# The last feed forward of a two-block network: seven of its eight upward weight groups as 2x2 block products, seven products for eight

## The reference, cut to what matters

```python
def squared_relu_mlp_2(h, w1, w2):
    return jnp.square(jax.nn.relu(h @ w1)) @ w2
...
        hx = modulate(rmsnorm(x, norm2_g[layer]), sh2, sc2)
        x = x + g2 * squared_relu_mlp_2(hx, w_mlp1[layer], w_mlp2[layer])
...
    return rmsnorm(x, final_g)
```

## Time and profile before

| | us |
|---|---|
| median of three runs | 3636.82 |
| lowest, highest | 3636.82, 3644.08 |
| span of the profiled execution | 3635.2 |
| PE busy in it | 3455.9 (95%) |
| the chain that ended last: PE's part | 88% |
| last feed forward, PE's part of the chain, 3253.80 to 3615.07 | 361.27 |
| ACT, DVE, POOL busy in the whole span | 1205.8, 2014.6, 226.8 |

### The profile page before, as it was taken

One profiled execution on the slowest core, in us unless ns is written; L12 is line 12 of the kernel. 1 busy time (PEld: TensorE's weight loads), 2 busy tenths in 40 slices (PEclk: granted clock), 3 DMA queues, 4 the chain that ended last, 5 costly groups with the idle time before them and its releaser, 6 DMA issues.

```text
span 3635.2 us, 42169 instructions
## 1 busy us (share of the span) xinstructions
PE 3455.9 (95%) x17456; PEld 2750.8 (76%) x17456; DVE 2014.6 (55%) x3705; ACT 1205.8 (33%) x2017; POOL 226.8 (6%) x314
## 2 busy tenths in 40 slices
PE   7989999999989999998999889999998998799998
PEld 6647688887867688887986567888886885478886
DVE  5564587896664578884125675333335235664334
ACT  5353432225453332223112233332333212243332
POOL 0200000001040000000000001000001000000000
PEclk9999999999999999999999799999999999889999
DMA  5302144442212154443210021122122310113331
GB/s 169 103 18 92 63 157 152 162 139 87 75 29 81 53 168 162 154 147 128 80 62 28 9 80 47 59 60 68 59 66 80 112 59 30 41 58 95 98 97 58
DMA packets 210011, 317.00 MB, mean 87 GB/s; under 512 B 5304, under 2 KB 154426, under 8 KB 208540
## 3 DMA queue, kind: packets, MB, share of 16 engines
q1 hardware_dynamic: 194012, 243.00, 20.8%
q0 software_dynamic: 15808, 71.31, 5.8%
HBM read 300.66 MB, written 14.49 MB: 87 GB/s over the span
## 4 chain that ended last, share of the span: by engine, by line
PE 88%; DVE 8%; ACT 3%; issue 1%; DMA 0%; SPq 0%; DVEq 0%; ACTq 0%
PE ps L94 87%; DVE t L115 4%; ACT t L100 3%; DVE t L107 2%; PE ps L97 1%; DVE t L111 1%; DVE t L125 0%; DVE t L121 0%; DVE ps L115 0%; DVE t L118 0%; DVE ps L107 0%; DMA t<-in_mem 0%; DVE t L112 0%; ACT L100 0%; DMA t<-in_ctx 0%
## 5 line engine op out<-in xcount | busy, mean ns | idle before, releaser
L94 PE MATMUL ps<-t,t 128*128 128x512 f32 (+6 forms) x17040 | 3401.5, 364 | 148.1 <-DVE t L115 67.6
L94 PEld LDWEIGHTS ps<-t,t 128*128 128x128 f32 (+3 forms) x17040 | 2700.6, 189 | 822.8 <-issue 168.6
L100 ACT ACTIVATE t<-t 128x1024 fp32r<-128x1024 f32 (+5 forms) x1158 | 819.5, 742 | 1256.6 <-PE ps L94 924.3
L107 DVE TENSOR_TENSOR t<-t,t 128x1024 fp32r<-128x1024 f32 (+6 forms) x790 | 724.6, 947 | 581.0 <-ACT t L100 575.3
L100 ACT ACTIVATE t<-ps 128x512 f32<-128x512 f32 (+7 forms) x442 | 222.5, 529 | 805.9 <-PE ps L94 767.5
L115 DVE SCALAR_TENSOR_TENSOR t<-t,t,t 128x256 f32<-128x256 f32 (+3 forms) x927 | 437.7, 535 | 13.6 <-ACT t L100 7.3
L107 DVE TENSOR_TENSOR t<-ps,t 128x512 f32<-128x512 f32 (+4 forms) x293 | 188.8, 661 | 206.1 <-PE ps L94 144.0
L115 DVE SCALAR_TENSOR_TENSOR t<-ps,t,t 128x512 f32<-128x512 f32 (+1 forms) x252 | 154.6, 661 | 254.6 <-PE ps L94 234.4
L107 POOL TENSOR_TENSOR t<-t,t 128x64 f32<-128x64 f32 (+1 forms) x208 | 143.4, 713 | 1721.1 <-ACT t L100 1576.0
L118 DVE COPY t<-ps 128x256 f32<-128x256 f32 (+3 forms) x162 | 73.0, 479 | 278.3 <-PE ps L94 259.7
L100 ACT ACTIVATE t<-t,t 128x512 fp32r<-128x512 f32 (+3 forms) x160 | 96.0, 603 | 194.0 <-DVE t L107 127.9
(11 more groups left out here) (33 smaller groups left out, 295.9 us busy)
## 6 DMA issues: line engine op xcount, KB each, us to landing
t<-in_w_ff SPq DMA_DIRECT2D x64, 1024.0 KB, 5.3
t<-in_w_mlp SPq DMA_DIRECT2D x64, 1024.0 KB, 5.4
t<-in_ada_w POOLq DMA_DIRECT2D x48, 1024.0 KB, 5.8
t<-in_w_in SPq DMA_DIRECT2D x30, 1024.0 KB, 5.3
t<-in_w_qkv_o SPq DMA_DIRECT2D x12, 1024.0 KB, 5.1
t<-in_w_mem_kv SPq DMA_DIRECT2D x8, 1024.0 KB, 7.1
t<-in_w_mem_q SPq DMA_DIRECT2D x8, 1024.0 KB, 5.1
t<-in_w_mem_o SPq DMA_DIRECT2D x8, 1024.0 KB, 5.1
```

What stands on the lines that cost most here:

```text
L94: return Issued(self, self.e and self.e.matmul(o, l, r, start=start, stop=stop, skip_group_check=True))
L100: return Issued(self, self.e and self.e.activation(o, i, f, **kw))
L107: return Issued(self, self.e and self.e.tensor_tensor(o, a, b, op))
```

## The change

Group 0 stays as it was in arithmetic (two units `first` of 48 matmuls of 512 columns). For each of groups 1 to 7, the 1024 x 512 weight is a 2x2 matrix of blocks a11, a12, a21, a22 of 512 x 256 (input half, output half), the 1024 x 512 activation a 2x2 matrix of halves of features and of tokens. The eight block products become seven, each of 2 output tiles x 4 k x 3 terms = 24 matmuls of 256 columns, with combined operands. PE runs them as `a11, s1, s2, a12, s3, s4, a22`.

What comes with it:

- Weight sums on POOL, four adds of 128 x 1024 a group (`w_sum`): s1 = a21 + a22, s2 = s1 + a11, s3 = a11 + a21, s4 = s2 + a12, read from the staging buffers into three buffers `SUM` (t134_182, t135_183, t136_184).
- Activation sums, once: four adds of 128 x 4 x 256 on POOL (`t_sum`), each then split by ACT (`t_high`) and DVE (`t_low`) into `T`. For that the normed activation is kept in float32 (`L1.H`), so the norm is now two instructions a k on ACT (shift in place, then the copy to the high part) and two on DVE.
- Operands are converted by halves of a block (items of 128 x 1024) into six slots in turn: per group seven items for the products and four for the downward step, 11 conversions on ACT and on DVE where there were 8. Item i waits until item i-6 has been used: a conversion stands behind the unit of PE's program that frees its slot. Items 2 and 3 are now converted ahead of the norm, 4 and 5 behind it.
- PSUM partial sums: a bank is copied by ACT twice a group (a11's into another bank, s1's into `SQ`), and DVE adds twice a group (behind s2 into a bank; behind s3 into `RS`). The four corners of the hidden tile go through Relu, Square, Copy as the four tiles did.
- SP loads a block when the items and the sums that read its buffer are done. The loads are the same 32 blocks in the same order.
- Downward: the same 96 matmuls a group, in four units of 24, two tiles each, in banks 0, 1 and 3, 4 by turns. A unit opens both of its banks at its start.

```diff
+            elif u[0] == "seven":
+                j, name = u[1], PRODUCTS[u[2]]
+                act.wait_ge("pr", j, u[2])
...
+                elif name == "s3":
+                    act.wait_ge("corner", j)
+                    corner(j, name, RS[1][:, :], -1.0)
...
+            for k in items_after(y):
+                high(k)
...
+        late = []
+        for y, u in enumerate(last_units):
+            if u[0] == "seven":
...
+                elif name == "s3":
+                    dve.wait_ge("pr", j, u[2])
...
+                    dve.tensor_tensor(RS[1][:, :], P[R1][:, :], SQ[1][:, :], ALU.add).then_inc("corner", j)
+            elif u[0] == "down":
+                for m in two(2 * u[2] + u[3]):
+                    dve.wait_ge("dn", u[1], m)
...
+            for v in late:
+                hidden_low(*v)
+            late = [(u[1], PRODUCTS[u[2]])] if u[0] == "seven" and PRODUCTS[u[2]] in CORNERS else []
+            for k in items_after(y):
+                low(k)
...
+        def w_sum(j, name):
+            n = [landing("up", j, b) for b in range(2)]
...
+            pl.wait_ge("landed", n[0])
+            pl.wait_ge("landed", n[1])
...
+        t_sum(0, half(h, 0, 0), half(h, 0, 0), half(h, 0, 1), ALU.subtract)
+        w_sum(1, "s1")
+        pl.wait_ge("nlo", "n2_1", 7, 0)
+        t_sum(2, half(h, 0, 1), half(h, 1, 1), half(h, 0, 1), ALU.subtract)
+        t_sum(1, half(h, 1, 1), half(h, 0, 0), half(h, 1, 1), ALU.add)
+        w_sum(1, "s2")
+        w_sum(1, "s3")
+        t_sum(3, half(h, 1, 0), half(h, 1, 1), half(h, 1, 0), ALU.subtract)
+        w_sum(1, "s4")
```

More of the change, by code:

```diff
@@ L483, in program @@
     H.CT, H.GS = ar([128, XR]), [ar([128, 256]) for _ in range(2)]
+    ar = Area(DYN + 2 * 8 * S * 4)
+    L1 = Tiles()
+    L1.T, L1.HID = ar([128, 4, 2, 4, 256], R), [place([128, 2, 4, S], R, YB), place([128, 2, 4, S], R, ar.at)]
+    L1.H = ar([128, 8, S])
+    i0 = U.out2[1][0].i % 2
+    slots = [ar([128, 2, 1024], R) for _ in range(2)]
+    slots += [place([128, 2, 1024], R, HLbase[(i0 + x // 2) % 2] + 8192 * (x % 2)) for x in range(4)]
+    L1.SUM = [ar([128, 1024]) for _ in range(3)]
+    SUM_OF = {"s1": 0, "s2": 1, "s3": 2, "s4": 0}
     ar = Area(D1)
@@ L582, in mixed_units, with half, item_source, items_after @@
         return out_
+    def half(x, k, t):
+        return x[:, 4 * k:4 * k + 4, 256 * t:256 * t + 256]
+    def item_source(k):
+        i = items[k]
+        if i[0] == "seven" and PRODUCTS[i[2]] in SUM_OF:
+            return L1.SUM[SUM_OF[PRODUCTS[i[2]]]][:, :], ("sum", i[1], PRODUCTS[i[2]])
+        if i[0] == "seven":
+            b, q = {"a11": (0, 0), "a12": (0, 1), "a22": (1, 1)}[PRODUCTS[i[2]]]
+            n = landing("up", i[1], b)
+        else:
+            q, n = i[3], landing("up" if i[0] == "first" else "down", i[1], i[2])
+        return STG[n % 2][:, 1024 * q:1024 * q + 1024], ("landed", n)
+    def items_after(y):
+        if y is None:
+            return []
+        return [k for k in range(6, len(items)) if item_done[k - 6] == y]
+    FORMS = {"a11": (0, 0), "s1": 0, "s2": 1, "a12": (1, 0), "s3": 2, "s4": (1, 1), "a22": 3}
+    R0, R1, R2, R4 = 6, 2, 7, 5
+    CORNER_BUF = {"a12": TMP[0][:, :], "s3": RS[1][:, :], "s4": TMP[1][:, :], "a22": SQ[0][:, :]}
+    BANK = {"a11": R1, "s1": R4, "s2": R1, "a12": R0, "s3": R1, "s4": R2, "a22": R1}
+    CORNERS = {"a12": (0, 0), "s3": (2, 256), "s4": (0, 256), "a22": (2, 0)}
     latent = [x for j in range(4) for x in (("k", j), ("q", 2 * j), ("q", 2 * j + 1))]
@@ L1812, in hybrid_scalar @@
         streams = [(X, S), (CX, C)][:len(segs)]
+        if l == 1:
+            return last_scalar(act, sq_free, rs_free, roots, project_out)
         project_out(U.out2[l], f"n2_{l}", streams)
@@ L2316, in vector @@
         dve.wait_ge("rs", ("fin", 0))
-        dve.wait_ge(*whole(U.ff2[1][1][7][1]))
+        dve.wait_ge("dn", 7, 7)
         for k in range(8):
@@ L2607, in hybrid_vector @@
         gla_low(len(sums) - 1)
+        if l == 1:
+            modulation(1, "n2_g1")
+            return last_vector(dve, newton, project_out, gain1)
         project_out(U.out2[l], streams, gain1, lambda m, z: ("ev", U.out2r[l][m // 4].n, m, z))
@@ L2818, in sync @@
         stream(len(blocks))
+        for x, (kind, j, b, src, kc) in enumerate(last_blocks):
+            n = len(blocks) + x
+            if x < 2:
+                sp.wait_ge("lo", n - 2, 1)
+            else:
+                kind_, j_, b_ = last_blocks[x - 2][:3]
+                if kind_ == "down" or j_ == 0:
+                    sp.wait_ge("wlo", item_of["down" if kind_ == "down" else "first", j_, b_, 1])
+                elif b_ == 0:
+                    for name in ("a11", "a12"):
+                        sp.wait_ge("wlo", item_of["seven", j_, PRODUCTS.index(name)])
+                    for name in ("s2", "s3", "s4"):
+                        sp.wait_ge("sum", j_, name)
+                else:
+                    sp.wait_ge("wlo", item_of["seven", j_, PRODUCTS.index("a22")])
+                    for name in ("s1", "s3"):
+                        sp.wait_ge("sum", j_, name)
+            sp.dma_start(STG[n % 2][:, :].rearrange("p (k n) -> p k n", k=kc), src).then_inc(s_stage[n % 2], "landed", n)
         for i in range(4):
```

290 lines of the change are left out of this document (286 added, 4 removed).

## The result

The changed kernel took **3660.82 us** (median of 4 runs, 3658.35 to 3663.27) where the kernel before took 3638.07 beside it: ratio 1.0058, 95% interval 1.0044 to 1.0072, slower. Timed again later it stood at 1.0046 (1.0033 to 1.0060). In us that is 17 to 21, where the forecast was 28.6.

What follows compares the result with a forecast made beforehand. The prediction took PE as the bound (busy 95% of the span, 88% of the chain). Its terms, -17.6 + 17.6 + 2.0 + 16.4 + 10.2 = +28.6 on 3636.8, gave 3665 us, range 3634 to 3683.

Steps and rivals of the forecast that it cites:

- the likeliest case: The forecast itself for the whole kernel: +28.6 us, 3665 us, own range 3657 to 3676, chance 0.45.
- PE's part: Sign to look for: PE's stretch from 3253.8 to its end grows from 361 to some 388 us.
- Products, -17.6: Groups 1 to 7: seven products take 19.9 us where a group took 22.4, saving 17.6 us in all.
- the rival of added-up weight loads: Weight loads bound the products, each taking 0.23 us: seven groups cost 117 us more, 3771 us; chance 0.01.
- POOL's add, 2.4: POOL's add of 128 x 1024, absent from the trace, takes 2.4 us by a straight line through shorter adds.
- First unit 4.2 late: Opening: PE ends its first unit at 3271.0 instead of 3266.85, +4.2 us; 1.7 without collisions.
- collisions: DVE operations with two SBUF inputs and POOL's adds go by turns: 2.3 us for an add, 1.1 for a split.
- Opening waits 13.4 and clock 2.0: Opening: PE waits 5.7 us ahead of s1 and 7.7 ahead of s2, 13.4; half clock there costs 2.0.
- Recurring waits 2.7 each, 16.4: Groups 1 to 6: PE waits 2.7 us for DVE's residual adds ahead of the third downward unit, 16.4 in all.
- split in the way: DVE's conversion behind product a12 stands first at the recurring place, bringing DVE to 1.4 us after product s3's end.
- Recurring clock, 10.2: Each of six recurring waits is followed by half clock on PE, costing 1.7 us each, 10.2 in all.
- rival of no clock loss: The recurring waits cost no clock, being in a dense PE stream: +18.4 us, 3655 us; chance 0.18.

Runs made afterwards that it cites:

- the second trace: The changed kernel run once more, unedited, for another trace and time: 3660.8 us, ratio 1.0046 to the kernel before.
- e5: Changed kernel with POOL's first activation sum and s1 sum started only when DVE has finished the norm: 3660.1 us, ratio 1.0046.
- e2: Changed kernel with POOL's s2 sum, in groups 2 to 7, waiting until DVE has split s1's sum: 3652.0 us, ratio 1.0031.
- e6: Kernel of e2 with DVE's split behind product a12 held until after s3's corner add: 3642.4 us, ratio 1.0002.
- e1: Changed kernel with DVE's split of the next s1 held until after the first downward unit's residual adds, groups 1 to 6: 3641.4 us, ratio 1.0001.
- e9: Changed kernel with residual adds ahead of the next s1 split, opening reordered, POOL's sums after the norm, buffers for two hidden tiles: 3631.8 us, ratio 0.9977.
- e10: Kernel of e9 with DVE's opening splits for s2 and a12 first, and ACT's bank copies ahead of s3 and s4 conversions: 3633.0 us, ratio 0.9975.

## Why the prediction was right, and where not

- **Direction and range: right**, 3660.8 within 3634 to 3683 and within the likeliest case's own 3657 to 3676, and by the mechanism named. The median is 4 us under the forecast, but part of this nearness is luck: the base was low (below), and by the ratios the excess is 17 to 21 us against 28.6. PE's part was to grow by some 27 us, from 361 to 388; it grew by 15.1, and by 18.5 in the second trace.
- **Products, -17.6: right.** Seven times 44.8 less 42.2 is 18.2. The 0.118 us a matmul from the earlier trace rows held with new weights each; the rival of added-up weight loads, 117 us, is refuted.
- **POOL's add, 2.4: right**, 2.45 alone, by the straight line through the shorter forms; the Trainium skill's figure ("GPSIMD Engine Reference", 3.1) gave 2.25 as an estimate. Beside DVE's splits it takes up to 3.4.
- **First unit 4.2 late: right in size**, 1.7 at its start and 2.4 in it. The 2.4 were all put down to collisions; taking these away gave back 1.85 (e5). The rest is clock, which was not in the term: PE ran at 0.50 for its first 5.3 us here and in e5, for 3.9 before. And what was given back was lost again at the two opening waits.
- **Opening waits 13.4 and clock 2.0: right in the sum, not in its parts.** Waits of 5.02 and 5.13 in place of 5.7 and 7.7, and clock 2.5 on s1 and 2.2 behind s2 in place of 2.0 in all: 14.9 against 15.4. That the sum came out is luck, since waits 3.3 us too long covered a clock loss 2.7 too small. Each of the two waits had its own slow stretch of 6.8 us, where the prediction let the first lie partly before the second wait.
- **Recurring waits 2.7 each, 16.4 (six times 2.7 is 16.2): right**, 15.07 measured, its two links shown by e2 (collision) and e6 (split in the way), its cause by e1.
- **Recurring clock, 10.2: the failed term.** The step was "Gaps as short as 2.76 and 2.41 us were followed by at least 3.3 us at 0.50 as well", read as if each of the six would be. The slow stretch had its size, but came behind 1 and 3 of six waits: some 1.7 and 4.7 us. A search of before's trace for more waits of that length would not have warned, since the one at 3063 is followed by 0.50 in every trace; the two rows are of other places, and ahead of that one PE streamed less. The prediction said so itself in its rival of no clock loss ("PE is dense on both sides here, in rows 9 it was not") and gave it 0.18. The truth lay between that rival (3655) and the forecast (3665), and so did eight of the nine executions (3658.4 to 3663.3; the ninth 3654.0).
- **The base.** The sum was set on a profiled execution of 3635.2 with little clock loss; 22 of the runs of before have a median of 3641.7. This lifts times, not the difference.

With measured sizes the first trace adds up: -18.2 + 4.1 + 14.9 + 15.1 + 1.7 = +17.6, against 16.7 between the traces.

## What to carry to other kernels

When a change adds a serial chain (load, sum, convert, split) to an in-order engine, look at what is queued behind the chain's last link and does not need it: two adds behind one split cost this kernel all that seven products in place of eight had saved. Ordering such consumers ahead is free; removing a collision or a delay inside a stretch where the same engine's row is full was no gain here (e5, e9, e10), since the gap moved to the next consumer. In this feed forward a wait of some 2.5 us on PE had to be priced at its length plus a part of a clock loss, and one of 5 us at its length plus the whole; how often such a wait costs clock is not to be taken over from another place of the trace.

## What the runs showed that was not expected

- The grant of 1.2 GHz behind a wait of 2.3 to 3.3 us in the dense stream differs between executions of one program (10 of 24 here, 1.3 to 1.8 us each); behind up to 1.75 it did not come in 12, behind 4.8 to 5.5 it came in all 6, for 1.4 to 2.8 us each. At another place of the same program a wait of 2.41 us had it in 14 of 14.
- Two traces of the same kernel differ by 5.25 us ahead of an untouched stretch, 3.2 of it at two stretches of half clock that one of them lacks, as much as an edit of this size is worth: parts of traces are to be compared from a common event.
- With full rows on both, POOL and DVE go on by turns of some 3.35 us a pair of 128 x 1024 operations, which alone take 2.45 and 1.22; a DVE operation of 512 columns, 0.69 to 0.75 alone, took 2.6 to 2.9 (DVE in e10 from 3267.6: 3.30, 3.33, 3.31 us; POOL there up to 3.37).
